# Samples' retention state in a decoder layer: tiled by sample and head with its read-out on VectorE, and a pooled unit split in two

## The reference, cut to what matters

```python
o = jnp.einsum('bhij,bhjd->bhid', att, vc) + jnp.einsum('bhid,bhde->bhie', qc * q_dec, s)
s = c_dec * s + jnp.einsum('bhjd,bhje->bhde', kc * k_dec, vc)
```

## Time and profile before

| | us |
|---|---|
| median of 3 runs | 1713.74 (1712.02 to 1720.97) |
| the profiled execution | 1713.25 |
| its span in the trace | 1711.4 |
| busy: TensorE | 1400.2 (82%) |
| busy: VectorE | 575.0 (34%) |
| busy: ScalarE | 281.5 (16%) |
| mean DMA rate | 348 GB/s |

### The profile page before, as it was taken

One profiled execution on the slowest core, in us unless ns is written; L12 is line 12 of the kernel. 1 busy time (PEld: TensorE's weight loads), 2 busy tenths in 40 slices (PEclk: granted clock), 3 DMA queues, 4 the chain that ended last, 5 costly groups with the idle time before them and its releaser, 6 DMA issues.

```text
span 1711.4 us, 24908 instructions
## 1 busy us (share of the span) xinstructions
PE 1400.2 (82%) x10783; PEld 869.5 (51%) x10783; DVE 575.0 (34%) x1253; ACT 281.5 (16%) x657; POOL 85.4 (5%) x115
## 2 busy tenths in 40 slices
PE   7999999999898999987777578776787676586675
PEld 6888788888666577733333233333333232232331
DVE  2845568678364111183420112110111110120114
ACT  0023210210443100121101102010120101011113
POOL 1220011111300000000000000000000000000000
PEclk9999999999898899998988789888898888888888
DMA  9975487686999799319999999999999999999995
GB/s 346 362 266 202 152 284 244 236 282 225 374 376 345 293 304 331 129 65 414 426 396 429 427 427 415 427 426 428 425 415 425 428 427 428 426 426 427 426 426 217
DMA packets 155125, 595.83 MB, mean 348 GB/s; under 512 B 9281, under 2 KB 115249, under 8 KB 121985
## 3 DMA queue, kind: packets, MB, share of 16 engines
q1 hardware_dynamic: 137648, 501.89, 74.2%
q0 software_dynamic: 10656, 76.25, 11.4%
q10 hardware_dynamic: 6704, 16.02, 2.4%
HBM read 585.07 MB, written 17.48 MB: 352 GB/s over the span
## 4 chain that ended last, share of the span: by engine, by line
DMA 38%; PE 23%; DVE 3%; ACT 1%; issue 1%; ACTq 0%; POOL 0%; DVEq 0%
DMA arena<-in_w_up 37%; PE ps L2074 9%; PE ps L2012 6%; PE ps L2092 3%; PE ps L2043 2%; DMA arena<-in_ln_b 1%; PE ps L2049 1%; PE ps L2003 0%; ACT arena L1550 0%; PE ps L2101 0%; DMA arena<-in_b_r 0%; PE ps L2123 0%; PE ps L2001 0%; PE ps L2230 0%; POOL arena L1510 0%
## 5 line engine op out<-in xcount | busy, mean ns | idle before, releaser
L2074 PE MATMUL ps<-arena 128*32 128x256 f32 x4352 | 346.6, 489 | 236.3 <-DMA arena<-in_w_up 232.2
L2074 PEld LDWEIGHTS ps<-arena 128*32 128x32 f32 x4352 | 184.7, 140 | 413.4 <-issue 366.9
L659 PE MATMUL ps<-arena 128*128 128x264 f32 x1664 | 381.7, 388 | 11.8 <-DMA arena<-in_w_in 11.8
L659 PEld LDWEIGHTS ps<-arena 128*128 128x128 f32 x1664 | 313.1, 191 | 64.3 <-issue 13.0
L1821 DVE TENSOR_TENSOR arena<-arena,ps 64x256 f32<-64x256 f32 x34 | 14.4, 424 | 470.4 <-ACT arena L1554 470.4
L2092 PE MATMUL ps<-arena 128*32 128x512 f32 x1088 | 125.1, 600 | 1.0 <-DMA arena<-in_w_down 0.7
L2012 PE MATMUL ps<-arena 128*128 128x264 f32 x512 | 120.9, 394 | 2.0 <-PEq L2294 2.0
L1554 ACT ACTIVATE arena<-ps 64x256 f32<-64x256 f32 x34 | 12.8, 375 | 587.4 <-PE ps L2074 587.4
L2012 PEld LDWEIGHTS ps<-arena 128*128 128x128 f32 x512 | 96.8, 192 | 24.4 <-issue 8.4
L2043 PE MATMUL ps<-arena 128*32 128x512 f32 (+1 forms) x816 | 98.5, 595 | 0.9 <-DVE arena L1773 0.9
L1567 ACT COPY arena<-ps 32x512 f32<-32x512 f32 x128 | 73.7, 576 | 129.4 <-PE ps L2092 128.3
(11 more groups left out here) (473 smaller groups left out, 1109.4 us busy)
## 6 DMA issues: line engine op xcount, KB each, us to landing
arena<-in_w_gate SPq DMA_DIRECT2D x60, 2048.0 KB, 31.1
arena<-in_w_up SPq DMA_DIRECT2D x60, 2048.0 KB, 34.2
arena<-in_w_down SPq DMA_DIRECT2D x60, 2048.0 KB, 31.4
arena<-in_w_in SPq DMA_DIRECT2D x52, 1024.0 KB, 6.4
arena<-in_w_o SPq DMA_DIRECT2D x16, 1024.0 KB, 10.9
arena<-in_w_down SPq DMA_DIRECT2D x8, 1024.0 KB, 29.3
arena<-in_w_up SPq DMA_DIRECT2D x8, 1024.0 KB, 32.8
arena<-in_w_gate SPq DMA_DIRECT2D x8, 1024.0 KB, 33.3
```

What stands on the lines that cost most here:

```text
L659: last = pe.matmul(ps[:, n % 2, 0:T], ring[:, slot, k, cols], x[:, k, :], start=(k == 0), stop=(k == KT - 1))
L2074: last = pe.matmul(ps[BS * q:BS * q + BS, 0, 0:CHUNK // 2], xs[:, kk * 4 + i, :], ring[:, s, at:at + CHUNK // 2], start=(k == 0), stop=(k ...
```

## The change

The state is tiled by sample and head. A unit u = 0 to 7 holds, on partition 64f + 8s + h (f = 0, 1), the eight state rows d = 64f + 8u to 64f + 8u + 7 of sample s and head h, each of 128 elements. So gamma, k and q are numbers of a partition (and row), and v is a row of the partition. Six matmuls at the sample phase's start turn k, q and v of the samples into that layout (`s_kqv`), and VectorE copies them (`k_row`, `q_row`, `v_row`). A unit on VectorE is then: k times v (L1036), s*gamma + that (L1038), times q (L1040), and added to `o_wide` (L1043, not for unit 0). After unit 7 a reduction (L1045) leaves 128x128, and one matmul with `halves` adds the two halves f. `new_outputs`, `values_in`, the scratch row of values and its copy are gone. A unit is loaded and stored by two DMAs of 64 partitions with 4 KB each.

Also moved: `peaks(0)` before `state(3)`; each unit from 4 on one step later; `state(6)` and `state(7)` behind the second half's maxima and shares; the read-out (`s_or`, `s_ft`) behind `fold(0)` and `values(6)`; the wait for `s_in` and `ret_out` behind `s_imp`; the stores of units 6 and 7, and with them `project_in(0)` and `(1)`, later in SP's program. And `pool_unit(31)` is split: its product before the wait for the last head's standard deviation, its sums behind the last `gated`.

```diff
-        ("gamma", np.tile(np.exp(log_g)[None], (P, 1))),
+        ("gamma", np.tile(np.exp(log_g)[:, None], (P // H, 1))),
...
-        pool.dma_start(m.ps_v.rearrange("s (h d) -> (s h) d", d=DH), rows[0:64, 0, :]).then_inc(S["s_kept"], 16)
...
             v.bn_aggr(agg[:, u, 0], stats[:, u, 0])
             v.bn_aggr(agg[:, u, 1], stats[:, u, 1]).then_inc(S["r_var"], 1)
+            if h == H - 1:
+                pool_product(N_UNITS - 1)
             v.wait_ge(S["r_std"], h + 1)
             done.link(v.reciprocal(rstd[:, u], rstd[:, u]))
...
-            kind, g = u // 16, u % 2
+            pool_product(u)
+            pool_sum(u)
+
+        def pool_product(u):
+            g = u % 2
...
             done.link(v.tensor_tensor(x4, x4, wsl[:, u // 2 % 2].unsqueeze(2).broadcast_to([P, 8, KV, DH]), ALU.mult))
+
+        def pool_sum(u):
+            kind, g = u // 16, u % 2
+            rows = gath[:, g]
...
-            units = 1 if 3 <= n < 3 + N_FRONT_UNITS or R_TILE < n < N_TILES and j not in (5, 6) else 0
+            units = 1 if 3 <= n < 3 + N_FRONT_UNITS or R_TILE < n < N_TILES - 1 and j not in (5, 6) else 0
...
+        assert pooled == N_UNITS - 1
+        pool_sum(pooled)
         v.sem_inc(S["pooled"], 1)
...
-    s_old, v_rep = [w(H, DH) for _ in range(3)], [w(H, DH)]
+    s_old, prod = [w(ND, DH) for _ in range(3)], w(ND, DH)
     w = Taker(arena, 12288, 16512)
-    v_rep.append(w(H, DH))
+    k_row, q_row, v_row = w(64), w(64), w(DH)
+    o_sum, halves = w(DH), w(64)
+    o_wide = view(m.cst, CP["dmask"][0], ND, DH)
     pt0 = w(1536)
     prob, probw, prob_c = w(2, CHUNK + 4), w(2, P + 4), w(256)
...
     w = Taker(arena, 22656, 24576)
...
     keys_t = w(2, 5, CHUNK)
...
+    cmpt, kct, imp8 = view(flat, 0, NBLK + 1, NBLK + 1), view(flat, 0, KV, KV * P), view(flat, 1620, 256)
     eqt = view(pt0, 0, NBLK + 1, NBLK + 1)
...
+    units = lambda t, u, f: t[:, :, 64 * f + ND * u:64 * f + ND * (u + 1), :].rearrange("s h d e -> (s h) (d e)")
...
-        def state_in(b):
-            sp.dma_start(s_old[b % 3], a["state"][b].rearrange("h d e -> d h e")).then_inc(st_in[b % 3], 16)
-
-        def values_in(b):
-            sp.dma_start(v_rep[b % 2].rearrange("p h d -> p (h d)"), m.ps_v[b:b + 1, :].broadcast_to([P, H * DH])
-                         ).then_inc(vr_in[b % 2], 16)
...
+        def state_in(u):
+            for f in (0, 1):
+                sp.dma_start(s_old[u % 3][64 * f:64 * f + 64].rearrange("p d e -> p (d e)"), units(a["state"], u, f)
+                             ).then_inc(st_in[u % 3], 16)
...
-        window_in(sp, a, m, 2)
-        sp.wait_ge(front["s_kept"], KEPT)
-        values_in(0)
-        values_in(1)
-        window_in(sp, a, m, 3)
-        window_in(sp, a, m, 5)
+        for b in (2, 3, 5):
+            window_in(sp, a, m, b)
+        def state_out(u):
+            sp.wait_ge(S["s_st_new"], u + 1)
+            for f in (0, 1):
+                sp.dma_start(units(o["s_ret"][0], u, f), s_old[u % 3][64 * f:64 * f + 64].rearrange("p d e -> p (d e)")
+                             ).then_inc(st_out[u % 3], 16)
+
         for b in range(NS_TOK):
-            sp.wait_ge(S["s_st_new"], b + 1)
-            sp.dma_start(o["s_ret"][0, b].rearrange("h d e -> d h e"), s_old[b % 3]).then_inc(st_out[b % 3], 16)
-            if b + 2 < NS_TOK:
-                values_in(b + 2)
+            if b < NS_TOK - 2:
+                state_out(b)
             if 1 <= b < NS_TOK - 2:
-                sp.wait_ge(st_out[(b - 1) % 3], 16 * ((b - 1) // 3 + 1))
+                sp.wait_ge(st_out[(b - 1) % 3], 32 * ((b - 1) // 3 + 1))
                 sp.wait_ge(S["s_st_o"], b)
                 state_in(b + 2)
             sp.wait_ge(S["s_turned"], 10 * (b + 1))
...
-        for n in range(3):
-            sp.wait_ge(st_out[n], 16 * len(range(n, NS_TOK, 3)))
-        sp.wait_ge(S["s_st_o"], NS_TOK)
-        project_in(sp, a, m, 0)
+        state_out(6)
         for b in (6, 7):
             sp.wait_ge(S["s_vst"], b - 5)
             window_in(sp, a, m, NS_TOK + b)
-        sp.wait_ge(S["s_scored"], 2 * NS_TOK)
+        state_out(7)
+        for n in range(3):
+            sp.wait_ge(st_out[n], 32 * len(range(n, NS_TOK, 3)))
+        sp.wait_ge(S["s_st_o"], NS_TOK)
+        project_in(sp, a, m, 0)
+        sp.wait_ge(S["s_osum"], 1)
         for n in range(1, N_EARLY):
             project_in(sp, a, m, n)
         sp.wait_ge(front["kv_out"], 160)
...
             if i == 0:
-                act.wait_ge(front["ret_out"], 16)
...
         exps(1)
         keep_out(0)
+        turned_probs(1)
         act.wait_ge(S["s_var"], 1)
         A.activation(std[0:64, :], agg[0:64, 1:2], ACT.Sqrt, bias=m.cst[0:64, CP["eps"][0]:CP["eps"][0] + 1]).then_inc(S["s_std"], 1)
-        turned_probs(1)
+        keep_out(2)
...
-        gam = s_("gamma").unsqueeze(2).broadcast_to([P, H, DH])
-
-        def state(b):
-            s, r = s_old[b % 3], v_rep[b % 2]
-            v.wait_ge(st_in[b % 3], 16 * (b // 3 + 1))
-            v.wait_ge(vr_in[b % 2], 16 * (b // 2 + 1))
-            v.tensor_tensor(s, s, gam, ALU.mult)
-            done.link(v.tensor_tensor(r, r, tr[:, G_RK, 8 * b:8 * b + 8].unsqueeze(2).broadcast_to([P, H, DH]), ALU.mult))
-            v.tensor_tensor(s, s, r, ALU.add).then_inc(S["s_st_new"], 1)
+        def state(u):
+            s, wide = s_old[u % 3], lambda row: row[:, ND * u:ND * (u + 1)].unsqueeze(2).broadcast_to([P, ND, DH])
+            done.link(v.tensor_tensor(prod, v_row.unsqueeze(1).broadcast_to([P, ND, DH]), wide(k_row), ALU.mult))
+            v.wait_ge(st_in[u % 3], 32 * (u // 3 + 1))
+            v.scalar_tensor_tensor(s, s, s_("gamma"), prod, ALU.mult, ALU.add).then_inc(S["s_st_new"], 1)
+            v.wait_ge(S["s_st_new"], u + 1)
+            v.tensor_tensor(prod if u else o_wide, s, wide(q_row), ALU.mult).then_inc(S["s_st_o"], 1)
+            v.wait_ge(S["s_st_o"], u + 1)
+            if u:
+                done.link(v.tensor_tensor(o_wide, o_wide, prod, ALU.add))
+            if u == ND - 1:
+                v.tensor_reduce(o_sum, o_wide.rearrange("p d e -> p e d"), AX_X, ALU.add).then_inc(S["s_osum"], 1)
 
...
-        v.wait_ge(front["ret_out"], 16)
...
+        v.tensor_tensor(halves, ident[:, 0:64], ident[:, 64:P], ALU.add)
+        v.wait_ge(S["s_kqv"], 1)
+        v.tensor_copy(k_row, ps[:, 4, 0:64])
+        v.tensor_copy(q_row, ps[:, 4, 64:P])
+        done.link(v.tensor_copy(v_row, ps[:, 4, P:2 * P]))
...
-        v.wait_ge(S["s_in"], N_IN)
...
+        v.wait_ge(S["s_in"], N_IN)
+        v.wait_ge(front["ret_out"], 16)
...
-        peaks(0)
-        state(4)
         top(0)
         negated(0)
+        state(4)
+        shares(0)
         state(5)
-        shares(0)
-        state(6)
         turned_probs(0)
-        state(7)
         peaks(1)
-        v.wait_ge(S["s_mxt"], 2)
-        v.tensor_copy(ot_r, ps[:, 3, 272:336]).then_inc(S["s_otr"], 1)
         top(1)
         negated(1)
+        state(6)
+        shares(1)
+        turned_probs(1)
+        state(7)
+        keep_out(1)
         v.wait_ge(S["s_or"], 1)
         done.link(v.bn_stats(stats[0:64, :], ps[0:64, 2, 0:DH]))
         v.bn_aggr(agg[0:64, :], stats[0:64, :]).then_inc(S["s_var"], 1)
-        shares(1)
...
-        turned_probs(1)
-        keep_out(1)
         keep_out(3)
...
 
-        def new_outputs(b):
-            pe.wait_ge(S["s_st_new"], b + 1)
-            for h in range(H):
-                q = 8 * b + h
-                last = pe.matmul(ps[:, 3, 272 + q:273 + q], s_old[b % 3][:, h, :], tr[:, G_RQ, q:q + 1], start=True, stop=True)
-            last.then_inc(S["s_st_o"], 1)
-
         def turn_peaks(h):
             pe.wait_ge(S["s_peak"], h + 1)
-            for b in ((2, 3), (6, 7))[h]:
-                new_outputs(b)
             pe.transpose(ps[0:2, 3, 0:P], mx[:, h, :], ident).then_inc(S["s_mxt"], 1)
...
         def turn_back(h):
             pe.wait_ge(S["s_top"], h + 1)
...
 
+        for f in (0, 1):
+            rows = ps[64 * f:64 * f + 64, 4]
+            pe.matmul(rows[:, 0:64], tr[:, G_RK, :], ident[:, 64 * f:64 * f + 64], start=True, stop=True)
+            pe.matmul(rows[:, 64:P], tr[:, G_RQ, :], ident[:, 64 * f:64 * f + 64], start=True, stop=True)
+            last = pe.matmul(rows[:, P:2 * P], tr[:, G_RV, :], ident, start=True, stop=True)
+        last.then_inc(S["s_kqv"], 1)
...
         turn_back(1)
         values(1)
-        pe.wait_ge(S["s_otr"], 1)
-        pe.transpose(ps[0:64, 2, 0:DH], ot_r, ident).then_inc(S["s_or"], 1)
         totals(1)
         values(2)
         turn_probs(1)
         values(3)
-        pe.wait_ge(S["s_gated"], 1)
-        pe.transpose(ps[:, 2, 256:320], o_n[0:64, :], id64).then_inc(S["s_ft"], 1)
         values(4)
         fold(0)
+        pe.wait_ge(S["s_osum"], 1)
+        pe.matmul(ps[0:64, 2, 0:DH], halves, o_sum, start=True, stop=True).then_inc(S["s_or"], 1)
         values(5)
         fold(1)
         values(6)
+        pe.wait_ge(S["s_gated"], 1)
```

(1 more changed line is left out.)

28 lines of the change are left out of this document (10 added, 18 removed).

## The result

The changed kernel takes 1698.94 us (median of 4 runs, 1696.1 to 1701.34); the kernel before, on the same chip, 1713.32 us (4 runs). The ratio is 0.9919, with a 95% interval of 0.9899 to 0.994: 14 us less, a gain of 0.8%. The forecast was 30 us less, 1683.5. The time lies inside the range of 1674 to 1701, but more than half of the expected gain is missing. The profiled execution takes 1701.34 us and spans 1699.6, so it is the longest of the four; its span is 11.8 us under that of before.

What follows compares the result with a forecast made beforehand. The prediction took the sample phase's TensorE and DMA engines as both near a bound, with gaps. 20.4 + 7.9 + 3.8 = 32.1 us, less 2.5 given back, is 29.6, taken as 30: 1713.5 - 30 = 1683.5 us, range 1674 to 1701.

Steps and rivals of the forecast that it cites:

- second view: Sample phase by stretches, 447.7 to 594.0 us: TensorE busy 124.9 of 146.3 us, DMA share 0.94; both near a bound.
- The one-column products: TensorE's L1185 products in the sample phase: busy 20.4 us, nothing beside them on TensorE, all of it goes.
- The waits before the maxima: TensorE's two waits for L1038, 9.8 us: first goes, 1.9 us of the second stays bare, 7.9 us saved.
- Rival 2: State's store-load loop: pair taking half as long again (11 us) returns 9 us; gain 21, 1692.5 us; chance 0.14.
- The last pooled unit: Sample phase's start: 4.4 us wait for the last gated goes, six matmuls take 0.6, so 3.8 us saved.
- VectorE's added work: State units on VectorE: 39.2 us for 29.3, each instruction 1.225 us; none of the extra 10 us on the path.
- rival 3: Change does little, within 8 us: VectorE's steps or a state load bare before each softmax step; 1710 us; chance 0.06.
- The sum up to values(0): Savings from the sample phase's start to values(0): 20.4 + 7.9 + 3.8 = 32.1 us earlier.
- What the end gives back: Between values(0) and the last fold, up to one page's time still due: 0 to 5 us returned, 2.5 taken.
- The check by volume: Sample phase's 43.9 to 46.0 MB at 396 to 428 GB/s: phase ends 24 to 37 us earlier.
- The pitch: State rows 64 KB apart might move at half rate: gain 2 to 15, taken as 10, 1703.5 us; chance 0.09.
- Chances: For the whole kernel: forecast's gain of 22 to 38 us 0.67; faster 0.87, same 0.09, slower 0.04.

Runs made afterwards that it cites:

- the kernel with the load first: Changed kernel with the load of state unit 4 moved ahead of the store of unit 2 in SP's program; ratio 0.9916 to the kernel before.
- the fourth buffer: Changed kernel with a fourth buffer for the state, in place of the front's rotation tables, so loads are asked for earlier; ratio 0.9900, median 1694.95 us.
- the trace with fewer broadcasts: Kernel before without six of its eight broadcasts of a sample's values, 3.1 MB less, engines' instructions unchanged; ratio 0.9973.

## Why the prediction was right at the start of the phase and wrong in its sum

**What bounds the kernel.** Right that the last phase keeps an earlier start: from the first projection to the end of the span it takes 1118.0 us (1699.6 - 581.58), before 1116.8 (1711.4 - 594.6). Wrong in the second view: "both are near a bound, with gaps". What the runs show is that bytes set the length more than TensorE's work: 4.2 MB less are worth 11 us in the changed kernel, 17.9 us less on TensorE 2.2 us in the one before.

**The one-column products, 20.4 us.** This is the step that failed. "All of it goes" is true of TensorE's rows and not of the time: taken out of the kernel before they give 2.2 us (interval 0 to 4.4), and put back into the changed one they cost 6. "Nothing runs beside them" was meant as an argument that they are on the path. But the loads ran beside them, and two of the places where they stood ended a wait for VectorE that itself waited for a load.

**The waits before the maxima, 7.9 us.** The first is gone, as expected, and the second is 2.99 us against the 1.9 that were to stay. But 5.16 us came new ahead of `turn_probs(0)`. Rival 2 named this loop and its condition: the pair of store and load was to take 22 us, half as long again would bring 9 us back. It took 17.6 and 17.2 us for unit 5 (488.46 to 506.01, to 523.2), 35 in all, 13 more; and for unit 4 the load alone took 23. Unit 4's wait, the larger, has another start that the prediction doesn't name: SP stood at the store of unit 2 until 488.46, though the load could go at 483.78 (the kernel with the load first). The measured 14.4 us lie in the 12 to 22 of rival 2, which had 0.14, and not in the forecast's 22 to 38. But the loop is not the whole of it: with the fourth buffer, where one wait of 4.9 us is left for the state, the ratio is 0.9900 and not the 0.9825 of the forecast.

**The last pooled unit, 3.8 us.** In the trace of TensorE's start it is as worked out (451.38). In the time it can't be resolved.

**VectorE's added work.** Right in size: 1.23 us for each instruction and 1.28 for the fused one, 5.0 us a unit. That nothing of it stands in TensorE's way held only for units whose load came in time: 3.8 us of unit 4 and 3.8 us of unit 5 stand bare ahead of the shares and the second maxima, as rival 3 had described it. With four buffers the first of these two waits is gone and the second is 2.0 us. Six matmuls took about 0.8 us (0.6 expected).

**The sum up to values(0), 32.1.** Measured 25 (535.04 against 560.0): the missing 7 are mainly the two waits, 5.16 and the 1.1 over what was to stay, and the slower clock behind the first of them (0.77 granted from 515 to 545 us), in which 20 transposes took 4.51 us (at 519.73) instead of 2.59.

**What the end gives back, 2.5.** Measured 12: from the end of `values(0)` to the last fold it is 44.5 us, before 32.5. With it the two differences make 13.1 where 29.6 were expected. This is the term of the sum that was mis-sized most. The reason given, that the queue isn't empty when `values(0)` ends, fits what was found, and was limited to one page's time. Three waits for windows (8.0 us in all) and `values` at half the clock stand there.

**The check by volume** had the answer and was mis-sized in one term. The bytes were right: 43.9 to 46.0 MB expected, 45.9 found. The rate was not. It took the best stretches, 396 to 428 GB/s, where the phase itself moved 343 at a share of 0.94, which stood in the earlier trace rows. At that rate 43.9 to 46.0 MB are 128 to 134 us, so the stretch that ended at 594.0 ends between 576 and 582, 12 to 18 us earlier. The changed kernel's ended at 581, 13 earlier. This is worked out after the fact, and the rate is no constant of the phase: it was 318 GB/s in the trace with fewer broadcasts, 332 with the products put back and 367 with four buffers. But a check that is made with the best rate can't contradict a sum.

**The pitch.** Given 0.09, with half the rate taken from a figure for 512 KB, and shown not to matter at 64 KB. **Chances.** A gain of over 0.5% was given 0.87, and it came. That the time fell inside the range says little for the forecast: the range had been drawn up to 1701 to take in rival 2, and the term of 20.4 us on which the forecast rested was not worth that.

**What stays open:** why 3.1 MB less give the kernel before only 4.6 us while 4.2 MB more cost the changed one 15 (in part SP's waits in that run); which parts of the change give the half of its gain that bytes and products together don't give; whether the form of the state's transfers, 64 partitions each, costs anything (theory F; SP's queue moved 17.75 MB at 41.7% of the engines in the phase, 318 GB/s at a full share, before 21.94 MB at 45.2%, 332); and what rate a full phase with this mix could reach. The fourth buffer moved 367 GB/s in its trace where 343 is usual, and its median is the lowest of the kernels that compute all, 1694.95 us (0.9900, interval 0.9877 to 0.9923), and again 0.9901 with windows on ScalarE's queue. It is faster than the kernel before; against the changed kernel the intervals overlap.

## What to carry to other kernels

Where the DMA engines are busy for nearly all of a stretch (here 0.94 of it), divide its bytes by no better rate than the stretch's own, and hold that against any sum along an engine. It is a bound and no forecast: for the six broadcasts it gave 8.9 us and 4.6 came. To see whether an engine's work is on the path, take it out of the kernel at hand in one run: here 17.9 us of it were worth 2. Do the same on the other side of the change: there the 64 products, 14 us more of busy TensorE, cost 6. And where each reordering turns one wait into another of the same length, stop reordering and count bytes.

## What the runs showed of the hardware

A gather to 64 partitions moved 250 GB/s at a full share, to 128 partitions 402 to 425. A DMA whose outermost dimension is 2 ran on two engines, at 53 GB/s for 0.5 MB pieces, and held up the windows behind it in SP's queue so that TensorE waited 29.2 us for one of them:

```profile
500.72 1.12 PE L1181 MATMUL ps<-arena 128*128 128x128 f32 x4 [29.23 <-DMA arena<-in_win_k]
```

Two queues with outstanding work shared the engines by packets at 488 to 500 us (268 and 270), so that the one with rows of 16 KB had four times the share of the one with rows of 4 KB. With rows of 4 KB in both it was 64.3 to 38.0%, at 765 and 450 packets. In the tail of the changed kernel TensorE, after its waits for windows, ran at half the full clock, which is the 1.2 GHz level; `values` of one sample then takes 3.64 us in place of 1.93:

```profile
565.00:575.00 10.00, 8.44 (x67) 3.38 (x71) 0.00 (x0) 0.21 (x1) 0.00 (x0) 0.50 0.64 188
```
